# A hybrid decoder layer's final LayerNorm: two of eight tiles scaled by ScalarE and added to bias rows that are already in the output

## The reference

```python
def layer_norm(x, g, b):
    mu = jnp.mean(xf, axis=-1, keepdims=True)
    xc = xf - mu
    var = jnp.mean(xc * xc, axis=-1, keepdims=True)
    y = xc * lax.rsqrt(var + LN_EPS) * g + b
...
m = grouped_moe(x, w_router, b_router, w_up[l], w_down[l])
x = layer_norm(DEEPNORM_ALPHA * x + m, ln2_g[l], ln2_b[l])
```

## Time and profile before

| | us |
|---|---|
| median of 3 runs | 1656.99 |
| lowest and highest | 1656.52 and 1657.79 |
| profiled execution | 1657.7 |
| its span, first to last instruction | 1656.0 |
| TensorE busy | 1589.0 (96%) |
| VectorE busy | 1179.1 (71%) |
| ScalarE busy | 845.5 (51%) |
| Pool busy | 185.5 (11%) |

### The profile page before, as it was taken

One profiled execution on the slowest core, in us unless ns is written; L12 is line 12 of the kernel. 1 busy time (PEld: TensorE's weight loads), 2 busy tenths in 40 slices (PEclk: granted clock), 3 DMA queues, 4 the chain that ended last, 5 costly groups with the idle time before them and its releaser, 6 DMA issues.

```text
span 1656.0 us, 20267 instructions
## 1 busy us (share of the span) xinstructions
PE 1589.0 (96%) x7715; PEld 1314.2 (79%) x7715; DVE 1179.1 (71%) x1479; ACT 845.5 (51%) x1176; POOL 185.5 (11%) x219
## 2 busy tenths in 40 slices
PE   8999999999999999999999997999999999999981
PEld 6788888888888888888788885788888888888770
DVE  3756868585666666332575677799999999998884
ACT  3013211215655555325221334688888888888773
POOL 0000000202212220000000001111111111111120
PEclk9999999999999999999999998999999999999995
DMA  5153535644332321411554567999999999999966
GB/s 168 39 106 47 135 68 84 82 93 132 90 103 83 104 84 52 151 47 45 173 174 121 174 219 275 341 378 374 367 361 365 349 361 342 351 353 362 356 228 217
DMA packets 159065, 329.30 MB, mean 199 GB/s; under 512 B 17999, under 2 KB 87631, under 8 KB 158970
## 3 DMA queue, kind: packets, MB, share of 16 engines
q1 hardware_dynamic: 142826, 289.70, 54.1%
q0 software_dynamic: 16144, 38.32, 7.7%
HBM read 296.75 MB, written 48.52 MB: 208 GB/s over the span
## 4 chain that ended last, share of the span: by engine, by line
PE 88%; DMA 6%; DVE 4%; issue 1%; ACT 1%; SPq 0%; DVEq 0%; POOLq 0%; ACTq 0%
PE ps L761 53%; PE ps L1100 26%; DMA e_raw<-in_w_down 3%; PE ps L876 2%; PE ps L861 2%; DVE e_lo L1960 2%; DMA e_raw<-in_w_up 2%; PE ps L1107 1%; PE ps L1041 1%; DMA x_raw<-in_x 1%; PE ps L1113 1%; DVE zout L2020 1%; DVE zout L2013 1%; DMA z_d<-ye,row_i 0%; PE ps L1008 0%
## 5 line engine op out<-in xcount | busy, mean ns | idle before, releaser
L1960 DVE TENSOR_TENSOR e_lo<-e_raw,e_hi 128x1024 fp32r<-128x1024 f32 x376 | 436.1, 1220 | 24.9 <-ACT e_hi L1422 20.6
L1422 ACT ACTIVATE e_hi<-e_raw 128x1024 fp32r<-128x1024 f32 x376 | 367.5, 1050 | 22.2 <-DMA e_raw<-in_w_down 15.8
L761 PE MATMUL ps<-xt_hi,w_hi 128*128 128x512 f32 x896 | 302.3, 394 | 1.7 <-ACT w_hi L1179 1.7
L761 PE MATMUL ps<-xt_hi,w_lo 128*128 128x512 f32 x896 | 298.1, 390 | 0.0
L761 PE MATMUL ps<-xt_lo,w_hi 128*128 128x512 f32 x896 | 298.0, 390 | 0.0
L761 PEld LDWEIGHTS ps<-xt_hi,w_lo 128*128 128x128 f32 x896 | 168.1, 188 | 35.7
L761 PEld LDWEIGHTS ps<-xt_hi,w_hi 128*128 128x128 f32 x896 | 167.8, 188 | 34.7 <-ACT xt_hi L1183 1.9
L761 PEld LDWEIGHTS ps<-xt_lo,w_hi 128*128 128x128 f32 x896 | 168.4, 188 | 33.0 <-DVE xt_lo L1525 0.2
L1558 DVE TENSOR_TENSOR w_lo<-w_raw,w_hi 128x512 fp32r<-128x512 f32 x136 | 95.0, 703 | 131.9 <-ACT w_hi L1179 128.5
L1179 ACT ACTIVATE w_hi<-w_raw 128x512 fp32r<-128x512 f32 x136 | 83.8, 628 | 203.4 <-PE ps L761 195.5
L1100 PE MATMUL ps<-e_hi,xe_hi 128*128 128x512 f32 x512 | 163.6, 401 | 8.5 <-DVE e_lo L1960 7.9
(11 more groups left out here) (302 smaller groups left out, 2250.0 us busy)
## 6 DMA issues: line engine op xcount, KB each, us to landing
e_raw<-in_w_up SPq DMA_DIRECT2D x128, 1024.0 KB, 21.7
e_raw<-in_w_down SPq DMA_DIRECT2D x64, 1024.0 KB, 21.4
w_raw<-in_w_in SPq DMA_DIRECT2D x64, 256.0 KB, 4.9
w_raw<-in_w_gate SPq DMA_DIRECT2D x48, 256.0 KB, 3.3
gates_d<-gate_t POOLq DMA_DIRECT2D x16, 512.0 KB, 3.3
gate_s<-gates_d SPq DMA_DIRECT2D x16, 512.0 KB, 3.6
qkv_d<-qkv POOLq DMA_DIRECT2D x12, 512.0 KB, 3.7
w_raw<-in_w_branch SPq DMA_DIRECT2D x24, 256.0 KB, 3.7
```

The lines of the kernel that those rows point to most:

```text
L761: last = nc.tensor.matmul(o(h, c1 - c0), st(k), mv(k, c0, c1), start=start and k == nk[0] and n == 0, stop=h in stop and k == nk[-1] and n ...
L1422: nc.scalar.activation(e_hi[:, (UPT + s) % RSPL, :], e_raw[r][:, s % 2, :], ACT.Copy).then_inc(e_h, 1)
L1960: nc.vector.tensor_tensor(e_lo[:, sp_, :], e_raw[raw_slot(b, s)][:, s % 2, :], e_hi[:, sp_, :], ALU.subtract).then_inc(e_all, 1)
```

## The change

Tiles 2 and 3 (SUMMED) are finished another way than the other six (PLAIN). SP waits for the gain and the bias to land and then stores lnb2, the bias in every row, to the output rows of tiles 2 and 3; these stores count on par9_in too. VectorE leaves out the second pass of the two tiles. ScalarE multiplies their zout by the reciprocal instead, both between its statistics of tile 5 and those of tile 6, and counts them on z_scaled. Pool, when its last scatter is issued, waits for the bias stores and for each copy, and stores the two tiles with a DMA that adds to what is in the output. SP's plain stores are six, on two semaphores instead of four, and at the end it waits for the two accumulating stores (out_sum) as well.

```diff
@@ -99,6 +99,9 @@
 STREAM += [("b", _t, 0) for _t in range(KT - 1, NBR * KT)]
 CE = CC + len(STREAM)
 POS = {_w: CC + _p for _p, _w in enumerate(STREAM)}
+
+SUMMED = (2, 3)
+PLAIN = (0, 1, 4, 5, 6, 7)
 
 
 def program(nc, x, w_in, b_forget, conv_w, conv_b, conv_ln_g, conv_ln_b, sc_w,
@@ -321,7 +324,7 @@
         th_ok, ht_h, ht_l, ye_ok, ye_out = sem("th_ok"), sem("ht_h"), sem("ht_l"), sem("ye_ok"), sem("ye_out")
         par9_in, x1s_ok, z_init = sem("par9_in"), sem("x1s_ok"), sem("z_init")
         z_mean, z_var, ln9 = sem("z_mean"), sem("z_var"), sem("ln9")
-        out_ok, out_dma = sem("out_ok"), [sem(f"out_dma{u}") for u in range(4)]
+        out_ok, z_scaled, out_sum, out_dma = sem("out_ok"), sem("z_scaled"), sem("out_sum"), [sem(f"out_dma{u}") for u in range(2)]
 
         std3, std6, std9 = sem("std3"), sem("std6"), sem("std9")
 
@@ -566,15 +569,19 @@
                 fetch_of(last_b, s, raw_slot(last_b, s), w_down[0, bass.ds(last_e, 1), s * P:(s + 2) * P, :])
             sp.dma_start(lng2[:], ln2_g[0].partition_broadcast(P)).then_inc(par9_in, 16)
             sp.dma_start(lnb2[:], ln2_b[0].partition_broadcast(P)).then_inc(par9_in, 16)
+            sp.wait_ge(par9_in, 32)
+            for t in SUMMED:
+                sp.dma_start(out[0, t * P:(t + 1) * P, :], lnb2[:]).then_inc(par9_in, 16)
 
             sp.wait_ge(ye_out, 16 * (last_b + 1))
             for t in range(TT):
                 sp.dma_start(zin[:, t, :], z_d[t * P:(t + 1) * P, :]).then_inc(tile_in[t], 16)
-            for t in range(TT):
-                sp.wait_ge(out_ok, t + 1)
-                sp.dma_start(out[0, t * P:(t + 1) * P, :], zout[:, t, :]).then_inc(out_dma[t % 4], 16)
-            for u in range(4):
-                sp.wait_ge(out_dma[u], 16 * TT // 4)
+            for n, t in enumerate(PLAIN):
+                sp.wait_ge(out_ok, n + 1)
+                sp.dma_start(out[0, t * P:(t + 1) * P, :], zout[:, t, :]).then_inc(out_dma[n % 2], 16)
+            for u in range(2):
+                sp.wait_ge(out_dma[u], 16 * len(PLAIN) // 2)
+            sp.wait_ge(out_sum, 16 * len(SUMMED))
 
 
         @block.gpsimd
@@ -748,6 +755,10 @@
                 gather(b)
             for k in range(3):
                 scatter(tail + 1 + k)
+            pool.wait_ge(par9_in, 16 * (2 + len(SUMMED)))
+            for n, t in enumerate(SUMMED):
+                pool.wait_ge(z_scaled, n + 1)
+                pool.dma_start(out[0, t * P:(t + 1) * P, :], zout[:, t, :], accum_op=ALU.add).then_inc(out_sum, 16)
 
 
         @block.tensor
@@ -1478,7 +1489,14 @@
 
             nc.scalar.activation(zst[:, 0, 5:6], eps[:], ACT.Sqrt)
 
+            def scale_z(t):
+                act.wait_ge(ln9, 2 * t + 3)
+                nc.scalar.activation(zout[:, t, :], zout[:, t, :], ACT.Copy, scale=zst[:, t, 4:5]).then_inc(z_scaled, 1)
+
             for t in range(TT):
+                if t == SUMMED[-1] + 3:
+                    for u in SUMMED:
+                        scale_z(u)
                 st = zst[:, t, :]
                 act.wait_ge(tile_in[t], 32)
                 nc.scalar.activation(st[:, 1:2], zin[:, t, D:D + 1], ACT.Copy, scale=-1.0 / D).then_inc(z_mean, 1)
@@ -2016,6 +2034,8 @@
                 st, z = zst[:, t - 1, :], zout[:, t - 1, :]
                 dve.wait_ge(std9, t)
                 nc.vector.reciprocal(st[:, 4:5], st[:, 3:4]).then_inc(ln9, 1)
+                if t - 1 in SUMMED:
+                    continue
                 dve.wait_ge(ln9, 2 * t + (t < TT))
                 nc.vector.scalar_tensor_tensor(z, z, st[:, 4:5], lnb2[:], ALU.mult, ALU.add).then_inc(out_ok, 1)
 
```

## The result

The changed kernel takes 1660.68 us (median of 20 runs, 1658.87 to 1662.82), the kernel before beside it 1657.78 us (20 runs, 1655.54 to 1658.99): a ratio of 1.0019, 95% interval 1.0013 to 1.0025, 2.9 us slower. That is within the 0.2% band of the prediction and by its own interval clearly not nothing. The forecast was +2.3 us.

A forecast was written before the change was run, and what follows sets the result against it. The prediction took VectorE's passes to pace the end before, and the DMA engines after: accumulations 2 x 4.0 plus plain stores 5.1 from 1644.2 end them 2.3 us later, 1656.99 + 2.3 = 1659.3 us; range 1654.5 to 1662.0.

The forecast's parts named there:

- VectorE, gain 2.3 us: Final LayerNorm: tiles 2 and 3 lose their second pass, 2.4 us, less a 0.1 us stall; VectorE ends 2.3 us earlier.
- ScalarE, two copies of 1.05 us, no stall to speak of: Before tile 6's statistics: two scaled copies of 1.05 us each, with a VectorE stall of 0.1 us allowed.
- Bias rows, 0: SP's two bias stores, near 1609.6 to 1612.2, are hidden: priced at 0, bound 0 to 0.8 us.
- Pool, first data at 1644.2: Pool's queue after the last scatter: tile 2's accumulating store, 0.56 us to issue, moves its first data at 1644.2.
- The sum: DMA work from 1644.2: two accumulations at 4.0 and four plain stores at 1.28 us end at 1657.3, span at 1658.3.
- The accumulating stores, the disputed price: Pool's two accumulating stores at the end hold the DMA engines 4.0 us each; bounds 3.4 and 6.2.
- break-even of 2.85: DMA engines at the end: the cost in us per accumulation at which the change equals the kernel before.
- the first rival: At the end, plain packets slip into gaps of the accumulations, so time follows VectorE: 1654.7 us; chance 0.16.
- the backlog: From the first plain store on, work queues up and the DMA engines don't rest, ending at 1657.3 instead of 1655.0.
- The span ends 1.0 us behind that: Program end: the span ends 1.0 us after the DMA engines stand still, as in the kernel before.
- The collision is hidden: Accumulations at the end cost other stores below 1.7 us each, so VectorE sets the end: 1654.7 us; chance 0.16.
- Dear accumulations: Accumulating stores at the end cost 4.5 us each or more, so time passes 1660.3, 1661.9 at 5.3; chance 0.27.

The follow-up runs named there:

- run 4: The changed kernel without bias stores and without Pool's two stores, so tiles 2 and 3 are never written: ratio 0.9979 to the kernel before.
- 7: The kernel before plus the two bias stores and SP's wait for gain and bias; plain stores overwrite the rows later: ratio 1.0010 to the kernel before.
- 10: The kernel before plus only SP's wait for gain and bias, no bias stores, as a null: ratio 0.9995 to the kernel before.
- 11: The kernel before plus the two bias stores and SP's wait, the same kernel as 7 timed again: ratio 1.0000 to the kernel before.
- 5: The changed kernel with ScalarE's copy of tile 2 moved ahead of tile 5's statistics, tile 3's left in place: ratio 1.0010 to the kernel before.
- 6: The changed kernel with tile 2 alone finished the new way, its copy ahead of tile 5's statistics: ratio 0.9995 to the kernel before.
- 9: The changed kernel with tiles 1 and 2 instead of 2 and 3, copies ahead of tiles 4 and 5: ratio 1.0003 to the kernel before.
- run 3: The changed kernel with Pool's two stores plain instead of accumulating, so tiles 2 and 3 lack their bias: ratio 0.9982 to the kernel before.
- 2: The kernel before with tile 7's plain store issued by Pool instead of SP: ratio 1.0032 to the kernel before.
- 8: The changed kernel without bias or accumulating stores; Pool adds the bias by tensor add, SP stores all tiles plain: ratio 1.0013 to the kernel before.
- 12: The kernel before with tile 5's plain store issued by Pool instead of SP: ratio 1.0014 to the kernel before.
- 1: The changed kernel with Pool also waiting for its own two accumulating stores before it ends: ratio 1.0034 to the kernel before.

## Why the prediction was right, and where by luck

The measured difference is 2.9 us where 2.3 was forecast, and 1660.68 lies in the range (the kernel before is itself 0.8 higher over 20 runs than over the three shown). But two of the steps were off, in opposite directions.

- **VectorE, gain 2.3 us**: right. Its last pass ends 2.4 us earlier from the first zin load, and run 4 shows the whole of it at the end of the program.
- **ScalarE, two copies of 1.05 us, no stall to speak of**: right, 2.17 us for both, and VectorE waited 0.18 us before tile 6.
- **Bias rows, 0**: they moved between 1610 and 1613, as said, and the scatter beside them took as long as before. Runs 7, 10 and 11 bound their cost at about 0.1%.
- **Pool, first data at 1644.2**: the reading behind it was off by two microseconds. What moved from 1645.5 on, 16.8 us behind the first zin load against a forecast 16.6, was tile 4's plain store; Pool's first packet moved only at 1647.2, 18.6 us behind that load. The sum lost nothing by it, since the engines were busy from 16.8 on. The issue of an accumulating store takes 0.96 to 1.08 us, not 0.56. Where nothing was in its way (runs 5, 6 and 9), the first packet moved 1.5 us behind the start of the issue.
- **"The accumulating stores, the disputed price", 4.0 us each**: mis-sized. It was 2.74 in the change, and 3.1 to 3.3 in runs 5, 6 and 9 (38.3% of 16 us for two in 5, 20.6% for one in 6, 39.9% for two in 9). That is under my lower bound of 3.4 and close to the break-even of 2.85 that the first rival named. The step took the scatters' rate per byte for that of rows that lie side by side; no run tells whether the order of the rows makes the difference, or what the scatter does for the slots that hold no token. The four plain stores took somewhat more than forecast, 36.0% of the 16 us to the end of the span, some 5.7 us instead of 5.1. So of the forecast 2.3 us from the backlog only 0.4 came, by the last packet and by the last landing.
- **"The span ends 1.0 us behind that"**: wrong, and this is the step that failed. I took the 1.0 us behind the last byte from the kernel before for a constant. From 0.9 behind the last packet it became 3.0 with Pool's stores late, because Pool's drain ends last. That supplied 2.1 us where the backlog fell short by 1.9, and so the sum came out. That the number is right is luck to this extent: of the 2.5 us by which the tail grew, 0.4 came the way that was forecast.
- **"The collision is hidden", 0.16**: its case was nearer than I had it, since a store took 2.74 us and not 4.0, but still above its 1.7. It did not come about, with or without the drain: the last landing came 5.5 us behind VectorE's last pass, against 2.7 before.
- **"Dear accumulations"**: not seen in any run, 3.3 us is the most.

How much each cause holds: with both stores plain (run 3) the tail is 4.7 us shorter. Of that the drain accounts for what ends last in both kernels, its end being 30.8 us behind the first zin load in the change and 26.0 in run 3. Pool's landing comes 4.7 us later with accumulation: its first packet moves 1.9 us later, behind tile 4's plain store, and from the first to the last packet of the two it is 6.9 us instead of 4.1, as two accumulations take 2.8 us more of the engines. So collision and drain are one chain: the accumulation makes Pool's landing late, and the drain hands it on with 4.9 us on top. Neither alone gives the +2.5: without the drain the last landing would end it at about +0.4, and without the collision (run 3) it is a gain.

The spans of the two profiles differ by 3.6 us, and 1.1 of them lie ahead of the tail. The runs give 2.9, and their interval, some 2.2 to 4.1 us, takes in the tail's 2.5 alone, so they do not show that any of the 1.1 belongs to the change. In the profile of the change TensorE's last block was 1 us longer, because the granted clock was at half (1.2 GHz) for longer after TensorE had stood still for 3.3 us. Before, in stretches of 1 us (PEclk is the third column from the end):

```profile
1613.00:1614.00 1.00, 1.00 (x3) 0.73 (x3) 0.00 (x0) 0.00 (x0) 0.00 (x0) 0.50 0.70 50
...
1616.00:1617.00 1.00, 1.00 (x5) 0.80 (x5) 0.00 (x0) 0.00 (x0) 0.00 (x0) 0.99 0.28 53
```

and after:

```profile
1611.00:1612.00 1.00, 0.17 (x1) 0.18 (x2) 0.69 (x2) 0.00 (x0) 0.60 (x1) 0.50 0.98 401
...
1616.00:1617.00 1.00, 1.00 (x4) 0.81 (x3) 0.00 (x0) 0.00 (x0) 0.00 (x0) 0.50 0.38 74
```

It was back by 1616 before and by 1617 to 1618 after. From the block's first matmul to ScalarE's next table load it was 8.8 us before and 9.7 after. In the profiles of the change and of runs 3, 5 and 9 it was 9.7 to 9.9, and 8.7 to 8.8 in those of before, 2, 4, 6, 7, 8, 10, 11 and 12: all four long ones are of kernels with both bias stores, but runs 7 and 11, with both as well, have it short. What goes with it is the moment at which the clock fell: in those four it fell 0.9 to 1.3 us before TensorE resumed, in the others at most 0.2 before, mostly after. Whether the change shifts this moment or it fell so by chance stays open.

## What to carry to other kernels

An engine that gives up work late is not enough: ask what each engine that gets new work does last, and what the program's end waits for behind it. Work that Pool gets late in a program can be paid again at the end: here the end came some 8.3 us behind Pool's last instruction or 4.9 behind the landing of its last DMA, whichever was later, also for a plain store and for a tensor add, where behind SP's stores it came 0.5 after the landing. And before work moves to a DMA that accumulates, count it at two to two and a half plain stores on the shared engines (2.74 to 3.3 us here, against 1.34).

## What the runs showed of the hardware that I had not expected

- Pool's drain at the end of the program ended 4.8 to 4.9 us behind the last landing of its DMAs (before, the change, runs 3 to 7, 9 to 11) but no sooner than 8.2 to 8.3 us behind its last issue, wait or tensor add (runs 1, 2, 8, 12). SP's took 7 ns, VectorE's 1.3 us, ScalarE's 0.3 us.
- A direct store of 0.524 MB from Pool held the DMA engines for 1.34 us plain (run 3) and 2.74 to 3.3 us accumulating (the change, runs 5, 6 and 9).
- A Pool tensor add of 128 x 1024 float32 beside VectorE's scalar_tensor_tensor of the same shape: 3.15 us for Pool's and 3.10 to 3.17 for VectorE's, which alone takes 1.28.
